# Prefix front without a normalised copy of x, another load order, and another order of work beside the down projection

## The reference, cut to what matters

```
mod = silu(c) @ w_ada + b_ada            # sh1, sc1, gt1, sh2, sc2, gt2 of 1024 each
h = rmsnorm(x, g_mix) * (1 + sc1) + sh1
x = x + gt1 * mixer(h)                   # short convolution, and an mLSTM with a running state
h = rmsnorm(x, g_ffn) * (1 + sc2) + sh2
x = x + gt2 * ((silu(conv3(h @ w_up_a)) * (h @ w_up_g)) @ w_down)
return rmsnorm(x, g_final)
```

## Time and profile before

| | |
|---|---|
| median of 3 runs | 1352.63 us (1352.62 to 1353.66) |
| profiled execution | 1352.54 us; span of its slowest core (5) 1351.2 us |
| spans of the 8 cores | 1340.9 to 1351.2 us |
| PE / VectorE / ScalarE busy on core 5 | 1258.2 (93%) / 684.6 (51%) / 538.7 us (40%) |
| granted TensorE clock, mean | 0.982 of full |

### The profile page before, as it was taken

The page is one execution under the profiler, slowest core; times in us unless marked ns, Lnnn a source line. Parts: engine busy times, 40 slices in busy tenths (PEclk is TensorE's granted clock), DMA queues, the critical chain, the costliest instruction groups (busy, mean ns, idle before and its releaser), DMA issues.

```text
span 1351.2 us, 21433 instructions; the slowest of 8 cores (1340.9 to 1351.2 us)
## 1 busy us (share of the span) xinstructions
PE 1258.2 (93%) x7662; PEld 690.8 (51%) x7662; DVE 684.6 (51%) x1251; ACT 538.7 (40%) x1081; POOL 76.0 (6%) x149
## 2 busy tenths in 40 slices
PE   0688999998989999999989999899999999999997
PEld 0346455666656655666644444445544444444443
DVE  0473342576823356665654413368723465656534
ACT  2465112665522225544433331466522245444202
POOL 1010000000100000000000000000000000000000
PEclk9898999998989999999999999999999999999999
DMA  9978024377593375334263674404437164532603
GB/s 178 234 187 142 10 40 84 51 119 129 97 203 57 69 144 107 63 63 79 40 133 73 177 141 79 77 15 80 101 87 125 23 135 93 91 65 33 108 2 124
DMA packets 35127, 130.37 MB, mean 96 GB/s; under 512 B 2764, under 2 KB 3020, under 8 KB 35024
## 3 DMA queue, kind: packets, MB, share of 16 engines
q0 software_dynamic: 24944, 93.74, 40.5%
q1 hardware_dynamic: 10080, 35.27, 7.8%
HBM read 214.34 MB, written 8.39 MB: 165 GB/s over the span
## 4 chain that ended last, share of the span: by engine, by line
PE 85%; DMA 5%; DVE 5%; issue 2%; ACT 2%; POOL 0%; DVEq 0%; SPq 0%; ACTq 0%; POOLq 0%
PE psum L509 56%; PE psum L1291 11%; PE psum L1146 4%; PE psum L805 4%; DMA wslot<-w_in 3%; PE psum L1387 2%; PE psum L714 2%; PE psum L485 2%; DMA arena<-xin 1%; DVE arena L994 1%; DMA arena<-bada_row 1%; ACT sqj L434 1%; PE psum L867 1%; PE psum L869 0%; PE psum L929 0%
## 5 line engine op out<-in xcount | busy, mean ns | idle before, releaser
L509 PE MATMUL psum<-arena,wslot 128*128 128x512 bf16 (+1 forms) x4640 | 830.2, 338 | 6.1 <-DVE arena L931 3.5
L509 PEld LDWEIGHTS psum<-arena,wslot 128*128 128x128 bf16 x4640 | 451.6, 98 | 354.8 <-issue 15.9
L1220 DVE SCALAR_TENSOR_TENSOR arena<-arena,pcol_t 128x1028 f32<-128x1028 f32 (+1 forms) x88 | 113.2, 1287 | 93.1 <-ACT arena L1217 88.2
L1291 PE MATMUL psum<-wslot,arena 128*128 128x512 bf16 x704 | 154.5, 382 | 1.5 <-ACT arena L489 1.5
L1082 ACT ACTIVATE arena<-psum,pcol_t 128x512 bf16<-128x512 f32 (+1 forms) x80 | 48.0, 603 | 163.1 <-PE psum L509 161.8
L1291 PEld LDWEIGHTS psum<-wslot,arena 128*128 128x128 bf16 x704 | 69.2, 99 | 85.2 <-issue 4.1
L434 ACT ACTIVATE sqj<-arena 128x1024 bf16<-128x1024 f32 (+1 forms) x49 | 51.7, 1055 | 142.0 <-DVE arena L1294 96.4
L1222 ACT ACTIVATE arena<-arena 128x1028 f32<-128x1028 f32 (+1 forms) x44 | 46.6, 1059 | 121.1 <-DVE arena L1220 121.1
L1094 DVE TENSOR_TENSOR arena<-psum,arena 128x512 f32<-128x512 f32 (+1 forms) x40 | 23.4, 586 | 83.4 <-PE psum L509 82.4
L1146 PE MATMUL psum<-wslot,arena 128*128 128x512 bf16 (+1 forms) x272 | 60.3, 379 | 0.2 <-DVE arena L493 0.2
L805 PE MATMUL psum<-wslot,arena 128*128 128x512 bf16 (+1 forms) x272 | 59.3, 379 | 0.0
(11 more groups left out here) (176 smaller groups left out, 1074.3 us busy)
## 6 DMA issues: line engine op xcount, KB each, us to landing
wslot<-w_in POOLq DMA_DIRECT2D x32, 1024.0 KB, 11.0
arena<-xin SPq DMA_DIRECT2D x32, 512.0 KB, 13.8
wslot<-w_ada POOLq DMA_DIRECT2D x12, 1024.0 KB, 13.1
wslot<-w_up_a POOLq DMA_DIRECT2D x10, 1024.0 KB, 10.6
wslot<-w_up_g POOLq DMA_DIRECT2D x10, 1024.0 KB, 12.2
wslot<-w_down POOLq DMA_DIRECT2D x8, 1024.0 KB, 9.0
y<-arena SPq DMA_DIRECT2D x16, 512.0 KB, 2.7
xt<-xin SPq DMA_DIRECT2D x15, 512.0 KB, 6.1
```

The lines of the kernel that those rows point to most:

```text
L509: S.op("pe", lambda e: e.matmul(psum[:, b, 0:n], lhsT=wv[:, k, wcol0:wcol0 + 128], rhs=src[:, k, t0:t0 + n], start=(k == 0), stop=(k == 7) ...
L1220: S.op("dve", lambda e: e.scalar_tensor_tensor(out=t3[:, T0:NT], in0=a_s[:, s_ + T0:s_ + NT], scalar=pcol[:, cw + s_:cw + s_ + 1], in1=t3[ ...
L1291: S.op("pe", lambda e: e.matmul(psum[:, b, :], lhsT=act_t[jj][:, t0:t0 + 128], rhs=wv[:, jj % 8, :], start=(jj == 0), stop=(jj == NFF - 1) ...
```

## The change

In the prefix, x is loaded straight as bfloat16 into `xnp` by GpSimd's queue and never scaled. The transposes evacuate G1 * x alone; the row's reciprocal root mean square (`rsP`) multiplies keys and gates as they leave PSUM. The shift sh1 enters as one row: sh1 (as two bfloat16 parts, broadcast to 128 columns, `shbc`) times the key and gate weights, added to keys (`bksh`) and gates (`gsh`). The order of loads on GpSimd's queue is: x tiles 0 to 3, two tiles of w_ada (sc1), key tile, x tiles 4 to 11, two tiles of w_ada (sh1), x tiles 12 to 15, query tile, value bias row. SyncE loads the tiles of stage 0 once x tile 13 has landed.

```diff
+        ask_prefix(0, 4, 2)            # x tiles c0..c1-1, then weight tiles up to the limit
...
+        ask_prefix(4, 4, 3)
+        ask_prefix(4, 12, 5)
+        ask_prefix(12, 16, 6)
+        S.dma("pool", bvbc[:], ...)
...
-        norm_upto(4, 4)
...
+        sumsq(0, 1, 2, 3)              # ScalarE: Square with sum, Sqrt of four; VectorE: reciprocal
+        banks0 = [transp_mm(tiles0, k) for k in range(6)]
         ada_cols(2)
         ada_cols(3)
-        ada_cols(0)
-        ask_x()
-        norm_upto(4, 4)
-        ada_cols(1)
         gain(G1, r_G1, 8, PC_GMIX)
+        for k in range(6):
+            transp_plain(tiles0, hTp[0], r_hTp[0], k, banks0[k])
...
+        def kevac(c, b):               # c < 8: kwp = psum * rs ; else kwp = psum * rs + bksh
+        def shift_row():               # 16 matmuls 128x512 and 16 of 128x8, two VectorE adds
...
+        S._wait("sp", dict([r_xnp[13].w]))
+        ask_x()
+        squares = {1: (4, 5), 2: (6, 7), 4: (8, 9), 5: (10, 11), 8: (12, 13), 9: (14, 15)}
         for c in range(NPF):
-            norm_upto(...)
+            norm_upto((0, 0, 0, 0, 0, 0, 0, 0, 0, 0, 1, 2, 3, 4, 5, 6)[c])
+            sumsq(*squares.get(c, ()))
             if c in (3, 7, 11):
                 tgroup(c // 4 + 1)
-            kproj(c)
+            b = kproj(c)
+            if c == NB:                # 8
+                shift_row()
+            kevac(c, b)
+            if c == NB - 1:
+                ada_cols(0)
+                ada_cols(1)
+                ...                    # shhl: sh1 in two parts; shbc: 128x2048 copy on VectorE
+            if c in (10, 12, 14, 15):
+                ...                    # VectorE: two tiles of keys + bksh, 128x1024 bf16
+        ...                            # gates: psum * rsP, then + gsh: four small VectorE instructions
```

The three groups of stage 0 evacuate three banks of eight on ScalarE and five on VectorE (before: four and four), and all norms left are done after the first group. Before the keys are weighted, VectorE makes `sdb`, the root mean squares broadcast to 128x2048, which takes the place of the tile of ones, and multiplies the weights by `rsP`:

```diff
+        S.op("dve", lambda e: e.tensor_copy(out=sdb, in_=sdP[:]...to_broadcast([128, NPF, 128])), ...)
+        S.op("dve", lambda e: e.tensor_tensor(out=wv_, in0=wv_, in1=rsP[:]...to_broadcast([128, NPF, 4]), op=ALU.mult), ...)
```

Beside the down projection of stage 0, six x tiles are loaded at once into six buffers (the four new ones are those of the up projection), and jobs and weight tiles are set out anew. The last chunk of stage 1 squares its first half of columns while i = 0 runs, and scales and stores in two halves:

```diff
-                    elif c in main[2:5]:
-                        dn_tile(1)
                     if jobs:
                         jobs.pop(0)()
+                    if i == 0 and c in (main[2], main[4], main[5]):
+                        dn_tile(1)
...
+            seq = [(norm, 0, 1), (), (norm, 2), (tr, 0), (norm, 3, 4), (norm, 5), (tr, 1), (norm, 6, 7), (), (tr, 2)]
...
+                        if last:
+                            sq1, r_sq1 = sumsq_half(xv, r_x1[c], 1)
+                            ...
+                            pieces = [(0, 512), (512, D)]
```

More of the change, by code:

```diff
@@ L277, in _build @@
         bkbc = at("E", 3 * 2048, [128, 512], BF16)
+        bksh = at("E", 7168, [128, 512], BF16)
+        shbc = at("F", 16384, [128, 16, 128], BF16)
+        gsh_t = sb("gsh", [128, 8])
+        ssqP, sdP, rsP = (sb(n, [128, NPF]) for n in ("ssqP", "sdP", "rsP"))
+        sdb = at("F", 16384, [128, NPF, 128], BF16)
+        gsh = gsh_t[:]
+        shhl = sb("shhl", [128, 16], BF16)
         xfr = [at("E", 8192 + i * 2048, [128, D], BF16) for i in range(4)]
@@ L289, in _build @@
         r_stat = RL("stat", 64)
-        r_ada1 = Res("ada1")
+        r_sq, r_sdP, r_rsP = RL("ssqP", 4), RL("sdP", 4), RL("rsP", 4)
+        r_bksh, r_shbc, r_gsh, r_shhl = Res("bksh"), Res("shbc"), Res("gsh"), Res("shhl")
         state = {"bank": 0, "xt": 0, "xnb": 0, "stat": 0, "slot": 0, "resv": set()}
@@ L715, in kproj @@
                      reads=[r_src[k], r_wslot[si_k]], writes=[r_bank[b]], inc=(k == 7))
-            S.op("dve", lambda e: e.tensor_tensor(out=kwp[0:p, c, :], in0=psum[0:p, b, :], in1=bkbc[0:p, :], op=ALU.add),
-                 reads=[r_bank[b], r_bk], writes=[r_kwp[c]])
             gate_mm(src, r_src, c, o, p, GBK)
-        tgroup(0)
+            return b
+        def kevac(c, b):
+            g, p = c // 4, psize(c)
+            rs = rsP[0:p, c:c + 1]
+            if c < NB:
+                S.op("dve", lambda e: e.tensor_scalar(out=kwp[0:p, c, :], in0=psum[0:p, b, :], scalar1=rs, scalar2=None, op0=ALU.mult),
+                     reads=[r_bank[b], r_rsP[g]], writes=[r_kwp[c]])
+            else:
+                S.op("dve", lambda e: e.scalar_tensor_tensor(out=kwp[0:p, c, :], in0=psum[0:p, b, :], scalar=rs, in1=bksh[0:p, :], op0=ALU.mult, op1=ALU.add),
+                     reads=[r_bank[b], r_rsP[g], r_bksh], writes=[r_kwp[c]])
@@ new lines, in shift_row @@
+        def shift_row():
+            b, b1 = next_bank(), next_bank()
+            for i in range(16):
+                S.op("pe", lambda e: e.matmul(psum[:, b, :], lhsT=shbc[:, i, :], rhs=wslot[si_k][:, i % 8, :], start=(i == 0), stop=(i == 15)),
+                     reads=[r_shbc, r_wslot[si_k]], writes=[r_bank[b]], inc=(i == 15))
+            for i in range(16):
+                S.op("pe", lambda e: e.matmul(psum[:, b1, 0:8], lhsT=shbc[:, i, :], rhs=wgate[:, i % 8, :], start=(i == 0), stop=(i == 15)),
+                     reads=[r_shbc, r_wgate], writes=[r_bank[b1]], inc=(i == 15))
+            S.op("dve", lambda e: e.tensor_tensor(out=bksh, in0=psum[:, b, :], in1=bkbc, op=ALU.add), reads=[r_bank[b], r_bk], writes=[r_bksh])
+            S.op("dve", lambda e: e.tensor_tensor(out=gsh, in0=psum[:, b1, 0:8], in1=pcol[:, PC_BG:PC_BG + 8], op=ALU.add), reads=[r_bank[b1], r_pc], writes=[r_gsh])
@@ L1360, in during_down, with load, norm @@
-            seq.append([end])
-            seq.append(late)
-            return [lambda fs=fs: [f_() for f_ in fs] for fs in seq]
+            bufs = [(xt[0][:], r_xt[0]), (xt[1][:], r_xt[1])] + [(xdn[i], r_xdn[i]) for i in range(4)]
+            tiles = [[] for _ in groups]
+            def load(c):
+                buf, r_b = bufs[c % 6]
+                S.dma("sp", buf, x_d[chunks[c][2]:chunks[c][2] + 128, :], writes=[r_b])
+            for c in range(6):
+                load(c)
+            def norm(c):
+                buf, r_b = bufs[c % 6]
+                j = state["xnb"]
+                state["xnb"] = (j + 1) % 4
+                tiles[c // 3].append((xnb[j], r_xnb[j], 128))
+                norm_to(buf, [r_b], xnb[j][:], r_xnb[j])
+                if c + 6 < len(chunks):
+                    load(c + 6)
@@ L1364, in _build, with tr @@
+            def tr(g):
+                transp(tiles[g], hT, chunks[groups[g][0]][0], r_h1[g], G1, r_G1, SH1)
+            seq = [(norm, 0, 1), (), (norm, 2), (tr, 0), (norm, 3, 4), (norm, 5), (tr, 1), (norm, 6, 7), (), (tr, 2)]
+            return [lambda q=q: [q[0](v) for v in q[1:]] for q in seq]
         hooks0["during_down"] = during_down
```

200 lines of the change are left out of this document (119 added, 81 removed).

## The result

| | before | after |
|---|---|---|
| median | 1352.72 us (1352.62 to 1353.66, 4 runs) | 1340.95 us (1339.36 to 1341.5, 4 runs) |
| ratio | | 0.9911, interval 0.9896 to 0.9927 |
| profiled execution; span of the slowest core | 1352.54; 1351.2 us (core 5) | 1341.2; 1339.8 us (core 2) |
| spans of the 8 cores | 1340.9 to 1351.2 us | 1330.5 to 1339.8 us |

The account below looks back on a forecast made before the run. PE's matmuls bound the body, VectorE next in the front: span 1351.2 - 14.9 (front) + 1.25 (prefix state) - 8.5 (down) - 0.6 (tail) = 1328.45, as a median 1329.9 us; range 1326 to 1333.

Parts of the forecast that it names:

- The stream of loads: Front: loads land at 6.48 us per 2.1 MB read; key tile at 32.9, sh1's second tile at 58.8.
- VectorE from there on: Front behind `shift_row`: VectorE works 31.0 us without a pause, PE needs 23; L509 starts at 97.6.
- Two signs of being wrong: Front: VectorE idle over 5 us in the last stretch; L509 starting before 92 or after 102.
- The front's sum: Front up to L509: 112.5 to 97.6, a gain of 14.9 us, at least 10, at most 26.
- VectorE isn't the bound: Front: PE or the loads bound it instead; L509 at 90, 7.6 earlier, time 1322; chance 0.23.
- The rival of a slower stream: Front: six load units at 7.2 us, sh1 4.3 later, slow clock 2 more; time 1336; chance 0.17.
- rival 4: Front: narrow cast packets of x's 2 KB rows make the kernel slower; 1360 at 4 us a tile; chance 0.03.
- The rule on GpSimd: Front: VectorE's fast two-port mode could delay six GpSimd load issues by 0.75 each, 4.5 us; forecast took nothing.
- The state of the prefix: Before the first prefix contraction: making `sdb` on VectorE adds 1.25 us to the path, ends 1.0 and 3.0.
- Down: Stage 0's down projection: both scaling stalls and the slow stretch go, gain 8.5 us (5.7 to 9); ScalarE's wait stays.
- Stage 1: Stage 1 up to its last matmul: no term in the sum, forecast difference 0.
- The tail: Last chunk: shorter square, split scaling and a half-size last store gain 0.6 us (0.5 to 1.1).

Follow-up runs that it names:

- the fastest version: Changed kernel, one store, tgroup first, query tile late, `sdb`/bksh additions moved, norms early, bias row behind x 15, two projections before stage 1's gates: 1328.46 us, 0.9814.

## Why the prediction was wrong

**The stream of loads: right in kind, 1.8 to 2.3 us late.** On core 2 kproj 0 started at 35.19 for 32.9 and the shift's second tile at 61.06 for 58.8; on the mean 34.2 and 60.6. The units themselves were right: from the key tile to sh1's second tile are four units, two of them x tiles, and they took 25.87 us for 25.9. Most of the lateness lies ahead of the key tile. Of the bias row, moving it showed 1.0 at the key tile and 2.1 at sh1's second tile, where I had 0.8: it makes 0.2 of the lateness at the first and 1.3 at the second. The new wait of PE for that tile came as forecast: 3.11 us. After it, kproj 8 was at the slow clock (3.44, I had 2.7; granted clock 0.54 of full), and VectorE's stretch began at 69.15 (mean 69.3) instead of 66.6.

**"VectorE from there on": the step that failed.** I added up 18.2 + 12.1 = 30.3 us of VectorE's work behind `shift_row` up to its last evacuation, and put nothing for pauses. On core 2, the slowest, the trace has 36.6 us there (69.15 to 105.7). Its pauses of 0.25 us and more sum to 7.0 (0.42, 0.27, 2.73, 1.68, 0.25, 1.00, 0.31, 0.31), which leaves 29.6 of work. Core 2 is the worst case; on the mean of the cores the stretch is 34.4 us, of which 4.5 are pauses (3.2 behind ScalarE, 1.3 behind PE) and 29.9 work. So the sum of the work was right, and that VectorE does it without a pause was not. Two signs of being wrong that I had named came true: pauses of over 5 us, on core 2, and the first projection after 102, on every core (102.9 to 106.3).

Two things that my text left out made the pauses. ScalarE too runs in order, and its squares stand ahead of evacuations that PE waits for. And I had stage 0's x tiles landing in time "as they are asked for", counting only how many, not what the one that ScalarE meets first waits for: it landed at 75.67, behind the query tile. Moving that tile gave 2.2, and the pauses fell from 4.5 to 2.6 with it. Moving tgroup ahead of the squares gave 1.0, at most half of it by the edit, and both with `sdb` early 2.9. The rest, 1.6 for the additions, 0.7 for the norms and 2.2 for the bias row, brought the front to 97.0 and, in the second run of the fastest version, 96.6.

That the front then ends where I had put it (97.6) doesn't bear the forecast out. It took six moves. Of the 7.9 us between 104.5 and 96.6, VectorE's stretch beginning sooner is 2.5, shorter pauses are 2.3, and 3.1 is work taken out of the stretch, most of it the additions. In the fastest version the stretch is 29.1 us, 26.8 of them work: there VectorE is nearly the bound that I had expected in the changed kernel.

**The front's sum.** On the mean: 2.7 for the late begin of the stretch, 4.5 for the pauses, less 0.4 of work, and 1.8 for counting from core 5: the 8.6.

**The rival "VectorE isn't the bound"** was right only in that VectorE wasn't the bound all the time. Its time was wrong: it had L509 at 90, and the front ended later than 97.6, not earlier, by chains through ScalarE. The rival of a slower stream had units of 7.2; they took 6.5, and what came late adds 2.7 of the 8.6. The narrow packets (rival 4) did nothing of the kind: the units with x tiles in them took 6.47 like the rest.

**The rule on GpSimd.** The changed kernel hardly puts it to the test. The Trainium skill ("SBUF — State Buffer", who interferes with whom) speaks of a VectorE instruction in a fast two-port mode, while GpSimd's issues from 35.60 to 41.70 us find VectorE idle, all but the last, which meets an evacuation of PSUM; the four x tiles among them took 0.53 to 0.56 us. Beside a copy from SBUF to SBUF three issues took 1.74 us, 0.58 each, and a weight tile's 0.71 beside the scaling of an x tile, 0.71 to 0.74 elsewhere. So no issue was longer by an instruction's 0.75, as in the earlier trace rows. Whether descriptors were written later for it can't be seen in these rows.

```profile
8.45 1.74 POOL L126 DMA_DIRECT2D arena<-xin  x3
8.77 0.76 DVE L419 COPY scolbc<-scol 128x1024 bf16<-128x1024 bf16 x1
...
36.77 0.56 POOL L126 DMA_DIRECT2D arena<-xin  x1 [0.45 <-issue]
...
89.47 0.71 POOL L126 DMA_DIRECT2D wslot<-w_in  x1 [43.93 <-DMA arena<-xin]
89.85 0.81 DVE L478 TENSOR_SCALAR arena<-arena,stat 128x1024 bf16<-128x1024 f32 x1
```

**The state of the prefix: right.** The pause before the contraction is 2.65 for 1.72, the stretch 1.04 longer; 1.25 was forecast, and the copy took 1.22 for 1.4.

**Down: right.** 7.9 us on the mean, 8.6 by taking the order back, for 8.5. Both stalls and the slow stretch went, and ScalarE's wait stayed as said (1.72).

**Stage 1: a second term that I put at nothing.** It has no term in my sum. PE waits 1.74 us for gm_logf, before and after, and the 16 matmuls behind it take 3.63 us on some cores and 5.31 on others: 5.31 on 1 core of 8 before, on none with the old down order, on 4 after, on 8 with the norms early, on 7 with the bias row late, and on 4 to 8 in all twelve versions with the new down order and the old stage 1. The cores with 5.31 are longer in the stage (before: 571.9 on that core, 569.9 to 570.1 on the others; after: 571.8 to 573.4 against 570.4 to 571.3). So with the new order more cores meet the lower clock there (one profiled execution of each version), and taking away the wait took the slow matmuls with it on every core of both executions, 3.2 us in all. What decides it core by core, with the same program and the same wait, stays open.

**The tail: wrong sign.** I had the first half of the store on its way 0.6 sooner and the last one half the size. The first came about (0.54 us sooner than the whole store on core 2), and the second half did land 2.0 us after its issue where a whole store takes 2.6. What I left out is the kernel's own order: the second half's store is issued only when the first has landed, so it starts 1.66 us later than the whole one (5.50 for 3.84). Two scalings also take 1.41 where one took 1.28. The shorter square made the scaling begin 0.33 us sooner (2.37 us after PE's last matmul for 2.70), and the one store land 0.34 sooner, but the span ends later behind that landing (0.52 us for 0.08), which none of the runs explains.

```profile
1334.27 1.41 DVE L1408 SCALAR_TENSOR_TENSOR arena<-arena,stat,gfinbc 128x512 f32<-128x512 f32 x2
```

The 12.5 us between forecast and mean (22.75 - 10.2) are thus 8.6 front, 1.6 tail, 1.3 stage 1, 0.6 down, 0.6 in the middle part, where nothing was changed and the scatter between cores is larger, less 0.2.

## What to carry to other kernels

When a sum says that an engine will be the bound, list for each of its instructions what it waits for, on every other in-order engine and in each DMA queue; a right sum of work with 13 to 19% of pauses is a wrong forecast. A load's place in the stream is priced by the first instruction that needs it and by all that is written behind that instruction: the same row of bias cost the front 2.2 us at the head of the stream, and moved behind the query tile it made the front 6.2 longer. It also takes one of the places that the kernel has for loads on their way. And undo each part of a joined change in turn, since a small one (the split store) can be a loss that the large ones hide; then look what it waits for, since here the loss was a wait that the kernel had written itself.

## What the runs showed of the hardware

- A broadcast row of 128x512 bfloat16 (0.131 MB written) at the head of GpSimd's queue held the key tile by 1.0 us and sh1's second tile by 2.1; at the queue's mean of 5.8 us/MB it would be 0.8. Why the second is twice the first is not shown.
- SyncE's loads are slowed by what GpSimd's queue holds: a 512 KB tile was used 11.2 us after it was asked for, and 6.8 us with a 1 MB tile out of the way.
- A store of half a tile (128x512 float32) landed 2.0 us after its issue, one of a whole tile 2.6 to 2.7: halving it saves 0.6, less than a wait for the other half costs.
- Behind the same wait of PE of 1.74 us, 16 matmuls took 5.31 us on some cores (mean granted clock 0.68 on core 2) and 3.63 on others (1.00 on core 1) within one execution, with the lower clock on none to all 8 of them, by version.
